# Attention scores of one layer: two float32r matmuls with split operands in place of one float32 matmul

## The reference, cut to what matters

```
q = rms_norm(q) * hd ** -0.5        # per head, with a gain
k = rms_norm(k)
s = einsum('bqhd,bkhd->bhqk', q, k) # the scores
s = s + c_t - c_s                   # c = cumsum(log_sigmoid(forget gate))
s = where(q_pos >= key_pos, s, -inf)
p = softmax(s); o = (p @ v) * sigmoid(o_gate)
```

## Time and profile before

| | busy us in the span | share |
|---|---|---|
| TensorE matmuls | 2905.2 | 97% |
| TensorE weight loads (beside the matmuls) | 2517.2 | 84% |
| VectorE | 1464.2 | 49% |
| ScalarE | 1101.7 | 37% |
| GpSimd | 211.3 | 7% |

### The profile page before, as it was taken

One profiled execution on the slowest core, in us unless ns is written; L12 is line 12 of the kernel. 1 busy time (PEld: TensorE's weight loads), 2 busy tenths in 40 slices (PEclk: granted clock), 3 DMA queues, 4 the chain that ended last, 5 costly groups with the idle time before them and its releaser, 6 DMA issues.

```text
span 2992.6 us, 46575 instructions
## 1 busy us (share of the span) xinstructions
PE 2905.2 (97%) x17931; PEld 2517.2 (84%) x17931; DVE 1464.2 (49%) x2102; ACT 1101.7 (37%) x1763; POOL 211.3 (7%) x177
## 2 busy tenths in 40 slices
PE   8999999999989999799999999999999999799998
PEld 7878879999989999799988888888888887588887
DVE  5555545555347776555543454453433335544422
ACT  4333334333235554333322223223344444332322
POOL 1000001000011221100001011011000000200000
PEclk9999989999999999899999999999999999899999
DMA  4222213332331111133333322322311112133332
GB/s 126 55 53 60 62 30 92 91 90 85 91 105 57 49 56 44 53 94 91 91 91 99 95 67 87 89 68 74 88 45 54 42 54 78 58 98 95 92 91 73
DMA packets 419559, 225.63 MB, mean 75 GB/s; under 512 B 7589, under 2 KB 416422, under 8 KB 419350
## 3 DMA queue, kind: packets, MB, share of 16 engines
q1 hardware_dynamic: 416438, 211.45, 24.4%
q0 software_dynamic: 2256, 10.32, 1.2%
q10 hardware_dynamic: 784, 2.75, 0.3%
HBM read 222.36 MB, written 2.13 MB: 75 GB/s over the span
## 4 chain that ended last, share of the span: by engine, by line
PE 62%; DVE 4%; issue 2%; ACT 1%; POOL 0%; DVEq 0%; ACTq 0%; POOLq 0%
PE ps L436 33%; PE ps L440 17%; PE ps L1038 2%; PE ps L854 2%; PE ps L996 1%; PE ps L1059 1%; PE ps L1027 1%; DVE wl L403 1%; PE ps L963 1%; PE ps L899 1%; PE ps L1031 0%; DVE rl L2143 0%; DVE xl L470 0%; DVE post_t L518 0%; DVE h L521 0%
## 5 line engine op out<-in xcount | busy, mean ns | idle before, releaser
L403 DVE TENSOR_TENSOR wl<-raw,wh 128x1024 fp32r<-128x1024 f32 (+4 forms) x429 | 518.8, 1209 | 401.6 <-ACT wh L399 398.0
L399 ACT ACTIVATE wh<-raw 128x1024 fp32r<-128x1024 f32 (+4 forms) x429 | 428.5, 999 | 729.7 <-PE ps L436 394.1
L440 PE MATMUL ps<-xh,wh 128*128 128x264 f32 x2736 | 571.4, 290 | 14.4 <-DVE xl L470 5.5
L440 PE MATMUL ps<-xl,wh 128*128 128x264 f32 x2736 | 559.4, 286 | 0.0
L440 PE MATMUL ps<-xh,wl 128*128 128x264 f32 x2736 | 559.1, 286 | 0.0
L440 PEld LDWEIGHTS ps<-xh,wh 128*128 128x128 f32 x2736 | 429.6, 190 | 24.3 <-issue 7.4
L440 PEld LDWEIGHTS ps<-xl,wh 128*128 128x128 f32 x2736 | 427.2, 189 | 0.0
L440 PEld LDWEIGHTS ps<-xh,wl 128*128 128x128 f32 x2736 | 425.9, 190 | 0.0
L436 PE MATMUL ps<-xh,wh 128*128 128x512 f32 x976 | 391.6, 401 | 17.7 <-DVE xl L470 14.0
L436 PE MATMUL ps<-xl,wh 128*128 128x512 f32 x976 | 387.8, 397 | 0.0
L436 PE MATMUL ps<-xh,wl 128*128 128x512 f32 x976 | 385.6, 395 | 0.0
(11 more groups left out here) (309 smaller groups left out, 4011.4 us busy)
## 6 DMA issues: line engine op xcount, KB each, us to landing
raw<-in_w_in SPq DMA_DIRECT2D x88, 512.0 KB, 4.0
raw<-in_ffn_w_gate SPq DMA_DIRECT2D x44, 512.0 KB, 3.8
raw<-in_ffn_w_up SPq DMA_DIRECT2D x44, 512.0 KB, 3.8
raw<-in_w_ffn_in SPq DMA_DIRECT2D x44, 512.0 KB, 3.8
raw<-in_fox_w_in SPq DMA_DIRECT2D x33, 512.0 KB, 4.1
raw<-in_hgrn_w_in SPq DMA_DIRECT2D x32, 512.0 KB, 3.9
raw<-in_ffn_w_down SPq DMA_DIRECT2D x32, 448.0 KB, 3.4
raw<-in_ffn_w_down SPq DMA_DIRECT2D x16, 512.0 KB, 3.7
```

The source lines that it names most:

```text
L399: nc.scalar.activation(wh[:, v % 2, 0:nk, :], raw[:, v % RAW_SLOTS, 0:nk, :], ACT.Copy).then_inc(s("w_hi"), 1)
L403: nc.vector.tensor_tensor(wl[:, v % 2, 0:nk, :], raw[:, v % RAW_SLOTS, 0:nk, :], wh[:, v % 2, 0:nk, :].bitcast(F32), ALU.subtract).then_in ...
L440: last = nc.tensor.matmul(ps[:, bank + b, 0:HALF], w[:, slot, kk, :], x[:, k0 + k, b * HALF:(b + 1) * HALF], start=first, stop=end_)
```

## The change

The scores become float32r matmuls. VectorE writes for each head a tile `q_p[:, b]` of 128 partitions: the rounded queries on the head's own 64 partitions and what rounding left (the rest) on the other 64. ScalarE writes `k_p[:, b]`: the rounded keys on both halves. VectorE writes `k_l`, the rest of the keys. One matmul with 128 rows of contraction gives (q rounded + q rest) x k rounded. A second one with 64 rows adds q rounded x k rest. The mask product uses float32r copies of `ident` and `future`, made once.

The calls move too. `qk_scaled` is split in two. `qk_scaled(i+1, 0)` and `query_parts(i+1)` now stand ahead of `o_t` on VectorE, while `qk_scaled(i+1, 1)` and `key_rest(i+1)` stand behind it. `key_parts(i+1)` stands behind `qk_rsqrt` on ScalarE, ahead of `yh` and `v_t`. Some semaphores are merged (`h_turned` and `ff_turned` into `turned`, `h_kept` and `ff_kept` into `kept`, `p_inv` and `gate_one` into `fox_step`) with the same order of work.

```diff
+    q_p, k_p = (a.take(n, [P, 2, L], F32R) for n in ("q_p", "k_p"))
+    k_l = a.take("k_l", [P, L], F32R)
+    ident_f, future_f = (a.take(n, [P, P], F32R) for n in ("ident_f", "future_f"))
...
                     for k0, k1 in runs:
-                        nc.tensor.matmul(flat[0:w, at + k0:at + k1], q_s[lo:hi, P * n:P * n + w],
-                                         k_s[lo:hi, k0:k1], start=True, stop=(k1 <= P * n))
-                    last = nc.tensor.matmul(flat[0:w, at + P * n:at + P * n + w], ident[:, 0:w],
-                                            future[:, 0:w], start=False, stop=True)
+                        nc.tensor.matmul(flat[0:w, at + k0:at + k1], q_p[:, b, P * n:P * n + w],
+                                         k_p[:, b, k0:k1], start=True, stop=False)
+                        nc.tensor.matmul(flat[0:w, at + k0:at + k1], q_p[lo:hi, b, P * n:P * n + w],
+                                         k_l[lo:hi, k0:k1], start=False, stop=(k1 <= P * n))
+                    last = nc.tensor.matmul(flat[0:w, at + P * n:at + P * n + w], ident_f[:, 0:w],
+                                            future_f[:, 0:w], start=False, stop=True)
...
-            pe.wait_ge(s("qn_done"), 2 * i + 4)
+            pe.wait_ge(s("qk_hi"), 2 * i + 2)
+            pe.wait_ge(s("qk_lo"), 2 * i + 2)
             scores(i, 0)
...
+        def key_parts(n):
+            act.wait_ge(s("qn_done"), 2 * n + 4)
+            copy(k_p[0:FOX_D, 0, :], k_s[0:FOX_D, :])
+            copy(k_p[FOX_D:P, 1, :], k_s[FOX_D:P, :]).then_inc(s("qk_hi"), 1)
+            copy(k_p[FOX_D:P, 0, :], k_s[0:FOX_D, :])
+            copy(k_p[0:FOX_D, 1, :], k_s[FOX_D:P, :]).then_inc(s("qk_hi"), 1)
...
             if ahead_:
                 qk_rsqrt(i + 1)
+                key_parts(i + 1)
             act.wait_ge(s("o_done"), i + 2)
...
+        def query_parts(n):
+            dve.wait_ge(s("qn_done"), 2 * n + 3)
+            V.tensor_copy(q_p[lo, 0, :], q_s[lo, :])
+            V.tensor_copy(q_p[hi, 1, :], q_s[hi, :]).then_inc(s("qk_lo"), 1)
+            dve.wait_ge(s("qk_lo"), 2 * n + 1)
+            V.tensor_tensor(q_p[hi, 0, :], q_s[lo, :], q_p[lo, 0, :].bitcast(F32), ALU.subtract)
+            V.tensor_tensor(q_p[lo, 1, :], q_s[hi, :], q_p[hi, 1, :].bitcast(F32), ALU.subtract)
+        def key_rest(n):
+            dve.wait_ge(s("qk_hi"), 2 * n + 1)
+            V.tensor_tensor(k_l[lo, :], k_s[lo, :], k_p[lo, 0, :].bitcast(F32), ALU.subtract)
+            V.tensor_tensor(k_l[hi, :], k_s[hi, :], k_p[hi, 1, :].bitcast(F32), ALU.subtract).then_inc(s("qk_lo"), 1)
+        V.tensor_copy(ident_f[:, :], ident)
+        V.tensor_copy(future_f[:, :], future)
...
             evacuate(1)
+            if ahead_:
+                qk_scaled(i + 1, 0)
+                query_parts(i + 1)
             dve.wait_ge(s("o_mm"), 2 * i + 2)
             dve.wait_ge(s("gate_ready"), i + 1)
             V.tensor_tensor(o_t[:, 0:SEQ], ps[:, 5, :], g_s[:, 0:SEQ], ALU.mult)
             V.tensor_tensor(o_t[:, SEQ:L], ps[:, 4, 496:512], g_s[:, SEQ:L], ALU.mult).then_inc(s("o_done"), 1)
             if ahead_:
-                qk_scaled(i + 1)
+                qk_scaled(i + 1, 1)
+                key_rest(i + 1)
```

More of the change, by code:

```diff
@@ L251, in program @@
     assert a.at <= yh_at
+    a = Area(rest, end)
+    q_p, k_p = (a.take(n, [P, 2, L], F32R) for n in ("q_p", "k_p"))
+    k_l = a.take("k_l", [P, L], F32R)
+    ident_f, future_f = (a.take(n, [P, P], F32R) for n in ("ident_f", "future_f"))
     a = Area(rest, end)
@@ L1113, in _ @@
                     if m >= 2:
-                        pe.wait_ge(s("h_kept"), 2 * m + g - 3)
-                    turned_out(lambda k: h[:, k, META:L], m, g, 4 + (2 * m + g) % 4).then_inc(s("h_turned"), 1)
+                        pe.wait_ge(s("kept"), 2 * m + g - 3)
+                    turned_out(lambda k: h[:, k, META:L], m, g, 4 + (2 * m + g) % 4).then_inc(s("turned"), 1)
             elif m == 4:
-                pe.wait_ge(s("h_kept"), KT)
+                pe.wait_ge(s("kept"), KT)
                 pe.wait_ge(s("ff_ready"), 4)
                 for c in range(NFULL):
-                    turned_out(lambda k: ff[:, k, :], c, 0, 4 + c).then_inc(s("ff_turned"), 1)
-        pe.wait_ge(s("ff_kept"), NFULL)
+                    turned_out(lambda k: ff[:, k, :], c, 0, 4 + c).then_inc(s("turned"), 1)
+        pe.wait_ge(s("kept"), KT + NFULL)
         for m in range(4, KT):
@@ L1131, in _ @@
                 mean.then_inc(s("ssum"), 1)
-        last.then_inc(s("ff_turned"), 1)
+        last.then_inc(s("turned"), 1)
     @block.scalar
@@ L1245, in _ @@
         qk_rsqrt(0)
+        key_parts(0)
         def pair_(i, ahead_):
@@ L1583, in _ @@
                 for g in range(2):
-                    act.wait_ge(s("h_turned"), 2 * m + g + 1)
-                    copy(o_tok[:, m, SEQ * g:SEQ * (g + 1)], ps[:, 4 + (2 * m + g) % 4, :]).then_inc(s("h_kept"), 1)
+                    act.wait_ge(s("turned"), 2 * m + g + 1)
+                    copy(o_tok[:, m, SEQ * g:SEQ * (g + 1)], ps[:, 4 + (2 * m + g) % 4, :]).then_inc(s("kept"), 1)
             if m == KT - 1:
@@ L1593, in _ @@
                 for c in range(NFULL):
-                    act.wait_ge(s("ff_turned"), c + 1)
-                    copy(f_tok[:, c, :], ps[:, 4 + c, :]).then_inc(s("ff_kept"), 1)
+                    act.wait_ge(s("turned"), KT + c + 1)
+                    copy(f_tok[:, c, :], ps[:, 4 + c, :]).then_inc(s("kept"), 1)
         act.wait_ge(s("ssum"), 8)
@@ L1787, in _, with qk_scaled @@
         own(V.tensor_scalar(span, floor, -1.0, 1.0, ALU.mult, ALU.add))
[L1789 to L1793, removed]
+        lo, hi = slice(0, FOX_D), slice(FOX_D, P)
+        def qk_scaled(n, j):
+            dve.wait_ge(s("qn_r"), 2 * n + j + 1)
+            V.scalar_tensor_tensor((q_s, k_s)[j][:, :], qk_raw[:, j, :], gains[:, ROW_QGAIN + j:ROW_QGAIN + j + 1],
+                                   post_t[:, j, :], ALU.mult, ALU.mult).then_inc(s("qn_done"), 1)
+        def query_parts(n):
[11 more added lines that the diff above has]
+        V.tensor_copy(future_f[:, :], future)
         scaled_out(PH_FOXP, 0, 1, qk_raw[:, 1, :])
@@ L1808, in _ @@
         scaled_out(PH_FOXP, 0, 3, v_s[:, :])
-        qk_scaled(0)
+        qk_scaled(0, 0)
+        query_parts(0)
+        qk_scaled(0, 1)
+        key_rest(0)
         def pair_(i, ahead_):
@@ L1826, in normalise @@
                 dve.wait_ge(s("p_exp"), 10 * i + 5 * b + 5)
-                V.reciprocal(rowinv[:, 5 * b:5 * b + 5], rowsum[:, 5 * b:5 * b + 5]).then_inc(s("p_inv"), 1)
-                dve.wait_ge(s("p_inv"), 2 * i + b + 1)
+                V.reciprocal(rowinv[:, 5 * b:5 * b + 5], rowsum[:, 5 * b:5 * b + 5]).then_inc(s("fox_step"), 1)
+                dve.wait_ge(s("fox_step"), 3 * i + b + 1)
                 for n in range(NTT):
@@ L1840, in gate @@
                 dve.wait_ge(s("gate_exp"), i + 1)
-                V.tensor_scalar(g_s[:, :], g_s[:, :], 1.0, None, ALU.add).then_inc(s("gate_one"), 1)
-                dve.wait_ge(s("gate_one"), i + 1)
+                V.tensor_scalar(g_s[:, :], g_s[:, :], 1.0, None, ALU.add).then_inc(s("fox_step"), 1)
+                dve.wait_ge(s("fox_step"), 3 * i + 3)
                 V.reciprocal(g_s[:, :], g_s[:, :]).then_inc(s("gate_ready"), 1)
@@ L2271, in _ @@
         dve.wait_ge(s("rstd_ready"), 8)
-        dve.wait_ge(s("h_kept"), KT)
-        dve.wait_ge(s("ff_kept"), NFULL)
-        dve.wait_ge(s("ff_turned"), NFULL + 1)
+        dve.wait_ge(s("kept"), KT + NFULL)
+        dve.wait_ge(s("turned"), KT + NFULL + 1)
         for c in range(NFULL):
```

## The result

The changed kernel takes 2976.29 us (median of 5 runs, 2975.36 to 2983.02); the kernel before took 2991.7 beside it (2991.58 to 2993.84). The ratio is 0.995, 95% interval 0.9939 to 0.9962: faster by 0.5%, 15.4 us, where 34.5 were forecast. The profiled execution took 2975.36 us, its span is 2973.7 us.

A forecast was written before the change was run, and what follows sets the result against it. TensorE, busy 97% of the span, was taken to bound the kernel. Fourteen looped calls at 2.19 us (30.7), pair 7 (4.8) and pair 0 (minus 1.0) save 34.5 us: 2959.8 profiled, median 2957, range 2936 to 2976.

The forecast's parts named there:

- I take 0.15, from the same instruction shapes at the same clock.: Scores on TensorE: each change between 64 and 128 contraction rows costs 0.15 us, eight such changes 1.20 us per call.
- the new call's 3.55 us: Predicted TensorE time of one new call of scores in the loop, where the old took 5.74: 2.19 us saved.
- 0.045: Tile 4 and its mask, 16 columns of weights: each change of rows costs 0.045 us, four per new call 0.18.
- its own range: The forecast's time with 0.12 to 0.2 us for a change of rows: 2948 to 2967 us.
- The clock falls in every pair: Rival, chance 0.05: late chain makes each looped pair wait and run at TensorE's lower clock, 86 us lost, time 3043.
- Pair 0 "minus 1.0": First pair: the new chain to the scores ends at 61.1, after TensorE wants it at 60.16; 1.0 us lost.
- Pair 7, 4.8 saved: Last pair, without group 0: two calls at the lower clock save 8.1 us, v_t comes 3.3 late, leaving 4.8.
- The loop's chain at nothing: Looped pairs: new VectorE and ScalarE work makes v_t 3.3 us later, still 0.9 us early, so it costs nothing.
- The chain is late in every pair: Rival, chance 0.16: new work delays the scores, 0.6 to 1 us lost in seven pairs; 25 us saved, time 2967.
- The time follows the passes alone: Rival, chance 0.20: changes of rows cost float32r nothing, a call takes 2.3 to 2.5 us; 53 us saved, time 2938.

The follow-up runs named there:

- e1: The changed kernel with the second product padded with zeros to 128 rows, so no change of rows in a call: 2932.9 us, ratio 0.9806.
- e4: The kernel before, float32 throughout, with 128 rows in every product, one head's keys beside zeros: 2960.7 us, ratio 0.9899.
- e3: The kernel before with only the mask product as float32r: 2995.1 us, ratio 1.001.
- e10: The changed kernel with v_t ahead of the key copies and keys scaled right behind the queries, changes of rows kept: 2970.3 us, ratio 0.9932.
- e12: The changed kernel with three float32r products of 64 rows per tile in place of one of 128 and one of 64: 2997.1 us, ratio 1.0011.
- e2: The changed kernel with all new VectorE and ScalarE work, but products and mask as the old float32 ones: 3004.7 us, ratio 1.0042.
- e6: e1 with ScalarE's copy of v (v_t) moved ahead of the four key copies: 2932.7 us, ratio 0.9798.
- e8: e1 with every product of a call cut into pieces of 128 columns: 2957.8 us, ratio 0.9882.
- e9: e6 with the keys scaled right behind the queries, ahead of query_parts: 2931.0 us, ratio 0.9795.
- e11: e4 with the mask product as float32r: 2951.3 us, ratio 0.9862.

## Why the prediction was wrong

Much of the mechanism held: TensorE's time is the kernel's in the loop, the changes of rows keep their price, the chain is hidden in the loop and shows at pairs 0 and 7. Two steps failed: the price of a change was too low, and the clock in the loop stood at nothing.

- **"I take 0.15, from the same instruction shapes at the same clock."** This is the mis-sized term. Of the new call's 3.55 us, the parts without changes (1.73 columns, 0.31 on top, 0.13 for weight loads) make 2.17, and e1 measured 2.18. The changes were put at 1.38 and are 1.85 to 1.87. The rows divide them. Up to the first matmul of tile 4 a call takes 3.12 us (161.19 to 164.31), and 1.67 in e1 (108.08 to 109.75): 1.45 for eight changes, 0.18 each. Tile 4 with its mask takes 0.91 us, and 0.51 in e1: 0.40 for four, 0.10 each, where the prediction had 0.045. So about half of what was missing lies in the eight and half in the four.

  In float32 the same reading (the earlier trace rows against e4: 4.60 and 3.14 us, then 1.14 and 1.04) gives 0.18 and 0.05: the 0.045 was about right for float32 and was carried over to float32r, where no row had it. The 0.15 was too low in both, because I charged 0.05 us per float32 matmul on top, from the earlier trace rows, where e4 shows 4.18 less 3.89 = 0.29 for eleven, 0.026 each. What I took away as a matmul's own cost belonged to the change. The better rows were already in the prediction: a float32 matmul of 128 columns takes 0.42 us with a change and 0.23 without, and the difference is 0.19.

  A pair without a stretch takes 43.60 us (47.14 less 3.54), so a call saves 1.77 instead of 2.19: 24.7 us in 14 calls, 5.9 short. (1.64 and 1.70 of it lie in a pair's two calls; a part of the other 0.2 us lies in the group between them, 5.96 us instead of 6.04.) The price of a change alone would have made the forecast 2963, still within its own range. (By 0.12 to 0.2 for a change alone that range is 2953 to 2964; its 2948 and 2967 hold pair 7's clock too.)
- **"The clock falls in every pair", 0.05.** The forecast's own sum had nothing for the clock in the loop, and the rival tied the fall to a wait of 1.65 us. It fell in four of seven pairs, in three of them without any wait, for about 3.4 us each, at 1.3 to 1.5 us a pair (45.06 to 44.93 less 43.60): 5.6 us. The rival had the wrong cause and a far higher price (10.7 us a pair on top of the wait). Stretches without a wait ahead of them showed in the loop of the four kernels whose float32r matmuls stand next to changes between 64 and 128 rows (after, e3, e10, e12), and in none of the others (before, e1, e2, e4, e6, e8, e9, e11; the one of e2 stands behind pair 0's wait). This is a correlation over one profile of each. In the two pairs of kernels that differ in hardly more than the rows of the scores, after and e1, e3 and e11, the stretches go with the changes; what in the chip makes it so is open. "TensorE: Matmul & The Clock Gate" of the Trainium skill, section HAM oscillation — how this bites in real kernels, puts a clock that falls again and again down to idle gaps of TensorE; here three of four stretches have no such gap, and the trace decides.
- **Pair 0 "minus 1.0".** The wait is 1.60 us and the scores start 1.7 later against the end of the setup. VectorE's subtractions follow each other at 0.72 us (0.63 assumed) and ScalarE's four copies take 2.63 (2.2).
- **Pair 7, 4.8 saved.** The wait is 5.51 (4.95 predicted), a call at the low clock 6.8 (6.2): 3.2 saved. The low level came as assumed, 0.51 from 371 to 389.
- **The loop's chain at nothing.** Right, by 0.25 us of cover: the rest of the 0.9 went to the same dearer copies. (With the full durations that the prediction names the chain grows by 1.0 us, 0.6 on VectorE and 0.4 on ScalarE, and not by 1.2.) "The chain is late in every pair" did not happen.
- **"The time follows the passes alone", 0.20.** Wrong for this kernel and right for e1: with no change of rows left, a call is 2.18 us and the kernel 2933, where that rival had 2.3 to 2.5 and 2938.

The ledger in the profiled executions: 24.7 in the calls, less 5.6 by the clock, less 1.7 at pair 0, plus 3.2 at pair 7, is 20.6 us in the Fox stage. The start of the kernel gives 0.8 more, and unchanged code behind the stage takes 2.4 back (1.7 of it in a stretch at 1.2 GHz from 2255 to 2260): 19.0 by the terms, against 18.9 between the two executions (2994.3 and 2975.36). The medians differ by 15.4. Of the 19 us that the forecast was off between the medians, 5.9 are the price of a change, 5.6 the clock in the loop, 2.3 pairs 0 and 7, 2.4 less 0.8 the rest of the kernel, and 3.5 the distances of the profiled executions from their medians.

For e1 the same ledger closes too: seven pairs at 7.24 us are 50.7, pair 7 gives 12.9 (two calls in 7.56 us, not 20.46) less 3.9 of wait, pair 0 takes 1.6, and the group behind the scores of pair 7 gives 1.7 (5.94 us instead of 7.66): 60 of the 61 us between the profiled executions.

## What to carry to other kernels

Count the changes of contraction rows in a stream of short matmuls before counting passes: here each cost about 0.18 us with 128 columns of weights, and padding a 64-row product with zeros to 128 rows took TensorE no extra time and gave some 30 us (float32, e4) or 43 us (float32r, e1). A cost found as a remainder is only as good as what was subtracted from it; ask for a row in which the same instruction stands without the suspected cause, and if there is none, widen the bounds. The clock can charge for a change where nobody waits (here 1.3 to 1.5 us in four of seven pairs), so the granted clock of every pair belongs in the reading, not that of the waits alone. The padding removed these stretches too.

## What the runs showed of the hardware beyond that

- In the looped pairs of the kernels with float32r matmuls and changes of rows, TensorE ran at 1.2 GHz for about 3.4 us at a time (about 7 us in four of e12's five), from late in a call or from its end on into the dense group, with TensorE busy in the records throughout and, but for pair 0, no wait ahead. Outside these four kernels the only such stretch in the loop is e2's, behind pair 0's wait.
- One wait of 1.58 us ahead of float32 scores with changes of rows brought 10 us at 0.53 of the clock (e2). Nearly the same wait ahead of other scores brought about 3.4 us (after, 1.60), about 7 us (e12, 1.60) or nothing (e1, 1.57, and e8, 1.58).
- ScalarE's copies of 64x528, two of the four onto other partitions, take what a copy of 128x528 takes: 2.63 us for four, 0.66 each, beside 0.65 for `yh`. VectorE's CAST of 64x528 takes 0.43.
